# A 16-column projection turned round: its weights stationary, all 256 tokens moving, the result copied out and transposed

## Chip, core and metric

The kernel runs on one core of one Trainium2 chip. The metric is the time of one execution on the device, in microseconds; the median over runs is compared.

## What is computed

Six transformer layers over 256 tokens of width 1024, all in float32. The last two layers (called 0 and 1 below) have a mixer of three branches. One of them is a state-space scan, whose time steps come from sixteen columns of the input projection:

```python
proj = h @ w_in[layer]                      # [256, 1024] @ [1024, IN_DIM]
gm_u, gm_v, ssm_z, ssm_xbc, ssm_dt, ... = split_cols(proj, IN_SIZES)   # ssm_dt: 16 columns
xbc = silu(causal_dwconv(xbc, conv_w, conv_b))
dt = softplus(ssm_dt + dt_bias)             # [256, 16]
y = ssd_scan(xs, dt, a_log, bm, cm, d_skip)
```

Everything in this document happens around `ssm_dt`, the product of 256 tokens x 1024 features with 1024 x 16 weights, once in each of the two layers.

## The kernel before

A float32 product is made of three F32R matmuls. Each operand is split into a high part (ScalarE copies it to F32R) and a low part (VectorE subtracts the high part from the original), and high x high, high x low and low x high are summed in PSUM. The weights stream in as tiles of 128 x 2048: SyncE loads `raw`, ScalarE makes `whi`, VectorE makes `wlo`. Three of each are kept, so the parts of a tile can be made when the tile three before it has been used.

The order of the work is written by a planner, class `Order`. It emits steps, and every engine runs those of its own that have the step's name, in this one order. A projection is a row of steps with a `yield` after each; at each yield `pump` runs, which puts in: a low part if one is due (every second pump), the next piece of the first generator in `pre`, and the next piece of the first generator in `side`. So the side work of the scan (generator `ssm`) is laid between the steps of the big projections, piece by piece. PSUM has eight banks; the side work takes banks 4, 5 and 6 in turn (`aux`), and a semaphore pair per bank (`full`, `empty`) orders writers and readers.

In each of the two layers the order around the change is: the projection of the convolution channels (`col` steps, result `b`), ScalarE's bias step `tap_b`, VectorE's convolution taps `taps_b` and ScalarE's `silu_b` in `pre`; the step `dt`; then the projection `u` (eight `col` steps of twelve matmuls, 256 moving columns each), with the pieces of `ssm` between: `softplus`, four `xs` transposes, `ends`, `cb`, `xde`; then the projection `z` (`tok` steps of six matmuls, 512 moving columns), with `mix`, `state`, `off`, `build`, `decay`, `diag` between.

Step `dt` of TensorE has, for each half of the tokens (t) and each of eight blocks of features (k), the three matmuls with the tokens stationary and the 16 weight columns moving. The result has tokens on the partitions, 16 columns per half, in one bank. VectorE's `softplus` waits for it, adds the bias (L2144), and goes back and forth with ScalarE (Exp, Ln) until `dt` (L2160) and `dA` (L2164) are there. Every line of a helper stands for many uses: L1073 to L1075 are `three`, L1078 is `mm`, L1082 is `tr` (a transpose through TensorE), L1139 to L1141 the matmuls of `col`, L1425 and L1429 are ScalarE's `act` and `copy`, L1768 is the low part of a weight tile, L2063 a convolution tap. In the names of the trace wdh and wdl are the high and low part of the sixteen columns' weights.

Of the kernel before, what the change touches and what calls it, by code (L numbers as in the profile page):

```python
# [164 lines left out]
class Order:  # L165
# [558 lines left out]
    def mixer_2(self, l):  # L724
# [58 lines left out]
        self.step("dt", l, x)  # L783

        def ssm():
            self.counts("stat_v", ("sp0", l))
            self.counts("stat_a", ("sp0", l))
            self.counts("stat_v", ("sp1", l))
            self.counts("stat_a", ("sp1", l))
            self.counts("dtv", l)  # L790
            self.counts("dav", l)
            self.step("softplus", l)
            yield
            for t in range(2):
                for q in range(2):
                    self.aux(("xs", l, t, q))
                    self.counts("xsg", (l, t, q))
                    self.step("xs", l, t, q)
                    yield
            self.aux(("ends", l))  # L800
            self.counts("ea", l)
            self.step("ends", l)
            yield
            self.aux(("cb", l))
            self.step("cb", l)
            yield
            self.counts("xde", l)
            self.step("xde", l)
            for _ in range(3):
                yield  # L810
            for g in range(2):
                self.aux(("state", l, g))
                self.step("state", l, g)
                yield
            for g in range(2):
                self.aux(("off", l, g))
                self.counts("offg", (l, g))
                self.step("off", l, g)
                yield
            seen["xn"] = True  # L820

            def build(n):
                self.counts("built", (l, n))
                self.step("build", l, n)
            build(0)
            yield
            for n in range(8 + 2):
                if n < 7:
                    build(n + 1)
                    yield  # L830
                if n < 8:
                    self.aux(("decay", l, n))
                    self.counts("decays", (l, n))
                    self.step("decay", l, n)
                    yield
                if 1 <= n < 9:
                    self.aux(("diag", l, n - 1))
                    self.step("diag", l, n - 1)
                    yield
# [221 lines left out]
def tensor_program(pe, o, B, sem):  # L1061
# [3 lines left out]
    def activation_ready(x, t, q):  # L1065
        b, n = use["turned", x, t, q]
        p.wait_ge(f"empty{b}", n + 1)
# [237 lines left out]
    def dt(l, x):  # L1305
        b, n = use["dt", l]
        p.wait_ge("wdl", mark["wdl", l])
        p.wait_ge(f"empty{b}", n)
        for t in range(2):
            for k in range(8):  # L1310
                activation_ready(x, t, k // 4)
                lh, ll = B.xh[:, k, 128 * t:128 * t + 128], B.xl[:, k, 128 * t:128 * t + 128]
                last = three(B.bank[b][:, 16 * t:16 * t + 16], lh, ll, B.wdh[:, 16 * k:16 * k + 16],
                             B.wdl[:, 16 * k:16 * k + 16], k == 0 and t == 0, k == 7)
        last.then_inc(sem[f"full{b}"], 1)

    def chan_ready(l, c0, c1):
# [83 lines left out]
    def yparts(l, t, q):  # L1401
# [3 lines left out]
        for k in range(4):  # L1405
# [2 lines left out]
        last.then_inc(sem[f"full{b}"], 1)  # L1408

    does = {"turn_x": turn_x, "tok": tok, "col": col, "row": row, "close": close, "parts": parts, "turn": turn,  # L1410
            "score": score, "probs": probs, "pv": pv, "opart": opart, "turned_up": turned_up, "dt": dt, "xs": xs,
            "ends": ends, "cb": cb, "state": state, "off": off, "decay": decay, "diag": diag, "mix": mix,
            "yparts": yparts}
    for what, *args in o.steps:
# [4 lines left out]
def scalar_program(ac, o, B, sem, ins):  # L1419
# [211 lines left out]
    def silu_b(l, n, j):  # L1631
# [7 lines left out]
            last = act(B.xb[:, c, :], B.xb[:, c, :], ACT.Silu)  # L1639
        last.then_inc(sem["xb"], 1)  # L1640

    def softplus(l):
        a.wait_ge("stat_v", mark["stat_v", ("sp0", l)])
        act(B.ea[:, :, :], B.dA[:, :, :], ACT.Exp).then_inc(sem["stat_a"], 1)
        a.wait_ge("stat_v", mark["stat_v", ("sp1", l)])
        act(B.ea[:, :, :], B.dA[:, :, :], ACT.Ln).then_inc(sem["stat_a"], 1)
# [90 lines left out]
    def mparts(l, j):  # L1737
# [8 lines left out]
            "qk_in": qk_in, "v_in": v_in, "turn": turn, "exp": exp, "probs": probs, "sink": sink, "merge": merge,  # L1746
            "opart": opart, "unturned": unturned, "silu": silu, "hhi": hhi, "tap": tap, "silu2": silu2,
            "gelu_v": gelu_v, "gm_squares": gm_squares, "setup": setup, "tap_b": tap_b, "silu_b": silu_b,
            "softplus": softplus, "xs": xs, "ends": ends, "state": state, "decay": decay, "gelu_u": gelu_u,
            "ya_hi": ya_hi, "z": z, "head_roots": head_roots, "rms_y": rms_y, "sigmoid": sigmoid,  # L1750
            "yparts": yparts, "mparts": mparts}
    for what, *args in o.steps:
# [4 lines left out]
def vector_program(ve, o, B, sem):  # L1757
# [378 lines left out]
                last.then_inc(sem[f"empty{b}"], 1)  # L2136

    def softplus(l):
        b, n = use["dt", l]
        dt, dA, ea, q = B.dt[:, :, :], B.dA[:, :, :], B.ea[:, :, :], B.qst[:, :, :]  # L2140
        v.wait_ge(f"full{b}", n + 1)
        v.wait_ge("small", 16 * (l + 1))
# [422 lines left out]
class Buffers:  # L2565


    def __init__(self, nc, ctx):
        def sb(name, shape, dt=F32, stack=ctx):
            return stack.enter_context(nc.sbuf_tensor(name, shape, dt))  # L2570
# [45 lines left out]
        self.wst = sb("wst", [128, 512])  # L2616
        self.wdh, self.wdl = sb("wdh", [128, 128], F32R), sb("wdl", [128, 128], F32R)
        self.dt, self.dA = sb("dt", [128, 2, 16]), sb("dA", [128, 2, 16])
        self.ea, self.am = sb("ea", [128, 2, 16]), sb("am", [128, 16])
        self.lamt = sb("lamt", [128, 8])  # L2620
        self.qst = sb("qst", [128, 2, 16])
# [184 lines left out]
```

## Time and profile before

| | |
|---|---|
| median of 3 runs | 2547.71 us (2542.21 to 2548.09) |
| profiled execution | 2540.47 us |
| its span, first to last instruction | 2538.6 us |
| TensorE busy (weight loads) | 94% (84%) |
| VectorE, ScalarE, GpSimd busy | 60%, 50%, 19% |
| mean granted TensorE clock | 0.972 of full speed |

The profile is of one execution. An engine's busy share is a mean over stages that have different limits. TensorE matmuls overlap in the pipeline, so what one costs is the distance from start to start and not its duration; the weight loads (PEld) have the clearer starts. A granted clock of 1.00 is 2.4 GHz, 0.50 is 1.2 GHz.

### The profile page before, as it was taken

The page shows a single profiled execution, that of the slowest core. Times are in us where ns is not written, and L with a number is a line of the kernel's source. Part 1 is how long each engine was busy: PE and PEld are TensorE (multiplying, and loading weights), DVE is VectorE, ACT ScalarE, POOL GpSimd, SP SyncE. Part 2 cuts the span into 40 slices and gives each one's busy share as a digit, 9 for nine tenths or more (in the row PEclk, how much of TensorE's full clock was granted, in tenths as well). Part 3 has the DMA queues.
Part 4 walks back from the last instruction along what each step waited for, and adds up shares of the span by engine and source line. Part 5 has one row for each costly group of instructions (what it writes and reads, how often), then busy time and mean ns, then how long its engine had stood idle before and what let it go on. Part 6 is the DMA issues. An engine that isn't in the chain of part 4 may idle for free.

```text
span 2538.6 us, 36912 instructions
## 1 busy us (share of the span) xinstructions
PE 2395.2 (94%) x15388; PEld 2128.6 (84%) x15388; DVE 1513.7 (60%) x2420; ACT 1260.2 (50%) x1806; POOL 481.9 (19%) x368
## 2 busy tenths in 40 slices
PE   7799999999899998999889979999999999989999
PEld 5589978787799777998669969888999898889898
DVE  5465455545654646556465467656677676566766
ACT  4344445455444455444444436555565565454654
POOL 3230042222400333003320001343100013431000
PEclk9799999999999999999889989999999999999999
DMA  6145543333355433555235533434454443344553
GB/s 247 50 171 186 192 166 117 124 142 117 143 189 189 176 133 141 199 183 185 77 117 199 188 140 133 149 121 150 167 186 179 182 163 140 130 150 166 181 185 133
DMA packets 58182, 398.94 MB, mean 157 GB/s; under 512 B 6816, under 2 KB 7072, under 8 KB 11680
## 3 DMA queue, kind: packets, MB, share of 16 engines
q1 hardware_dynamic: 56864, 393.75, 43.0%
q8 instruction: 122, 2.00, 0.3%
q10 hardware_dynamic: 1152, 2.83, 0.3%
q14 instruction: 44, 0.36, 0.0%
HBM read 395.51 MB, written 1.05 MB: 156 GB/s over the span
## 4 chain that ended last, share of the span: by engine, by line
PE 78%; DVE 11%; ACT 7%; issue 2%; POOL 2%; DMA 0%; DVEq 0%; SPq 0%; ACTq 0%; POOLq 0%
PE b L1139 12%; PE b L1141 12%; PE b L1140 12%; PE b L1073 11%; PE b L1074 11%; PE b L1075 11%; PE b L1078 6%; PE b L1082 3%; DVE wlo L1768 3%; ACT whi L1429 2%; ACT S L1426 2%; DVE b L1792 1%; DVE st L1849 1%; DVE b L1847 1%; DVE xl L1799 1%
## 5 line engine op out<-in xcount | busy, mean ns | idle before, releaser
L1768 DVE TENSOR_TENSOR wlo<-raw,whi 128x2048 fp32r<-128x2048 f32 x351 | 831.2, 2373 | 451.4 <-ACT whi L1429 450.6
L1429 ACT ACTIVATE whi<-raw 128x2048 fp32r<-128x2048 f32 x362 | 691.0, 1910 | 355.8 <-PE b L1141 225.9
L1139 PE MATMUL b<-xh,whi 128*128 128x256 f32 x2560 | 727.1, 284 | 3.1 <-DVE wlo L1768 3.1
L1140 PE MATMUL b<-xl,whi 128*128 128x256 f32 x2560 | 722.2, 282 | 0.0
L1141 PE MATMUL b<-xh,wlo 128*128 128x256 f32 x2560 | 722.0, 282 | 0.0
L1139 PEld LDWEIGHTS b<-xh,whi 128*128 128x128 f32 x2560 | 486.1, 190 | 7.9 <-DVE wlo L1768 3.7
L1140 PEld LDWEIGHTS b<-xl,whi 128*128 128x128 f32 x2560 | 486.3, 190 | 2.0
L1141 PEld LDWEIGHTS b<-xh,wlo 128*128 128x128 f32 x2560 | 485.7, 190 | 0.0
L1073 PE MATMUL b<-whi,xh 128*128 128x512 f32 x832 | 345.0, 415 | 32.8 <-DVE xl L1799 16.2
L1074 PE MATMUL b<-wlo,xh 128*128 128x512 f32 x832 | 330.7, 397 | 0.0
L1075 PE MATMUL b<-whi,xl 128*128 128x512 f32 x832 | 329.9, 397 | 0.0
L1073 PE MATMUL b<-whi,oh 128*128 128x512 f32 x656 | 265.4, 405 | 5.6 <-DVE wlo L1768 5.6
L2321 POOL TENSOR_TENSOR wlo<-raw,whi 128x2048 fp32r<-128x2048 f32 x11 | 50.7, 4611 | 1148.1 <-ACT whi L1429 1148.1
L1074 PE MATMUL b<-wlo,oh 128*128 128x512 f32 x656 | 261.5, 399 | 0.0
L1075 PE MATMUL b<-whi,ol 128*128 128x512 f32 x656 | 260.8, 398 | 0.0
L1073 PEld LDWEIGHTS b<-whi,xh 128*128 128x128 f32 x832 | 157.6, 189 | 80.6 <-issue 21.4
L1075 PEld LDWEIGHTS b<-whi,xl 128*128 128x128 f32 x832 | 157.1, 189 | 38.5
L1074 PEld LDWEIGHTS b<-wlo,xh 128*128 128x128 f32 x832 | 157.9, 190 | 33.8 <-issue 1.9
L1073 PEld LDWEIGHTS b<-whi,oh 128*128 128x128 f32 x656 | 127.0, 194 | 32.4 <-DVE wlo L1768 6.9
L1075 PEld LDWEIGHTS b<-whi,ol 128*128 128x128 f32 x656 | 126.3, 192 | 27.7
L1074 PEld LDWEIGHTS b<-wlo,oh 128*128 128x128 f32 x656 | 126.5, 193 | 24.3
L1425 ACT ACTIVATE S<-b 128x256 f32<-128x256 f32 (+1 forms) x104 | 43.4, 418 | 175.8 <-PE b L1141 128.4
(225 smaller groups left out, 2833.6 us busy)
## 6 DMA issues: line engine op xcount, KB each, us to landing
raw<-in_w SPq DMA_DIRECT2D x362, 1024.0 KB, 4.8
gt<-in_rows SPq DMA_DIRECT2D x8, 512.0 KB, 4.0
bt<-in_rows SPq DMA_DIRECT2D x8, 512.0 KB, 5.0
abq<-in_rows ACTq DMA_DIRECT2D x2, 768.0 KB, 5.4
x<-in_x SPq DMA_DIRECT2D x1, 1024.0 KB, 6.7
bc<-in_rows SPq DMA_DIRECT2D x4, 256.0 KB, 5.1
out<-x SPq DMA_DIRECT2D x4, 256.0 KB, 2.0
msk<-in_masks SPq DMA_DIRECT2D x1, 768.0 KB, 7.7
```

The lines of the kernel that those rows point to most:

```text
L1073: pe.matmul(out, lh, rh, start=start, stop=False, skip_group_check=True)
L1074: pe.matmul(out, lh, rl, start=False, stop=False, skip_group_check=True)
L1075: return pe.matmul(out, ll, rh, start=False, stop=stop, skip_group_check=True)
L1078: return pe.matmul(out, l, r, start=start, stop=stop, skip_group_check=True)
L1082: return pe.transpose(out, i, B.ident[0:n, 0:n])
L1139: pe.matmul(out, wh[:, k, cs], ah[:, kk, :], start=kk == 0 and s == 0, stop=False, skip_group_check=True)
L1140: pe.matmul(out, wh[:, k, cs], al[:, kk, :], start=False, stop=False, skip_group_check=True)
L1141: last = pe.matmul(out, wl[:, k, cs], ah[:, kk, :], start=False, stop=final and k == 3, skip_group_check=True)
L1426: return ac.activation(out, i, f, bias=bias, scale=scale, accum_out=acc)
L1429: return ac.activation(out, i, ACT.Copy)
L1768: ve.tensor_tensor(B.wlo[s][:, :], B.raw[r][:, :], B.whi[s][:, :], ALU.subtract).then_inc(sem["loV"], 1)
L2321: ge.tensor_tensor(B.wlo[s][:, :], B.raw[r][:, :], B.whi[s][:, :], ALU.subtract).then_inc(sem["loG"], 1)
```

## The change

The operands of the `dt` matmuls are exchanged. The weights (128 features x 16 columns) are stationary, and all 256 tokens move, so the halves of the tokens fall together: 24 matmuls in place of 48, and the result has the 16 columns on the partitions and the tokens along the row. It must be turned back. ScalarE copies the 16 x 256 values out of PSUM into a new buffer `dtT` (a new step of its own at the place of `dt`), and TensorE transposes the two halves of it into another bank (step `dt_turn`), from which `softplus` now reads. The `ssm` generator begins with a `yield` more, and `dt_turn` and `softplus` stand together after it, so all pieces of `ssm` stand one pump later than before. One use more of `aux` turns the rotation of banks 4, 5, 6 by one from there on.

```diff
--- before.py
+++ after.py
@@ -783,6 +783,9 @@
         self.step("dt", l, x)
 
         def ssm():
+            yield
+            self.aux(("dt_turn", l))
+            self.step("dt_turn", l)
             self.counts("stat_v", ("sp0", l))
             self.counts("stat_a", ("sp0", l))
             self.counts("stat_v", ("sp1", l))
@@ -1307,11 +1310,20 @@
         p.wait_ge("wdl", mark["wdl", l])
         p.wait_ge(f"empty{b}", n)
         for t in range(2):
-            for k in range(8):
-                activation_ready(x, t, k // 4)
-                lh, ll = B.xh[:, k, 128 * t:128 * t + 128], B.xl[:, k, 128 * t:128 * t + 128]
-                last = three(B.bank[b][:, 16 * t:16 * t + 16], lh, ll, B.wdh[:, 16 * k:16 * k + 16],
-                             B.wdl[:, 16 * k:16 * k + 16], k == 0 and t == 0, k == 7)
+            for q in range(2):
+                activation_ready(x, t, q)
+        for k in range(8):
+            ks = slice(16 * k, 16 * k + 16)
+            last = three(B.bank[b][0:16, 0:256], B.wdh[:, ks], B.wdl[:, ks], B.xh[:, k, :], B.xl[:, k, :], k == 0, k == 7)
+        last.then_inc(sem[f"full{b}"], 1)
+
+    def dt_turn(l):
+        b, n = use["dt_turn", l]
+        bd, nd = use["dt", l]
+        p.wait_ge(f"empty{bd}", nd + 1)
+        p.wait_ge(f"empty{b}", n)
+        for t in range(2):
+            last = tr(B.bank[b][:, 16 * t:16 * t + 16], B.dtT[:, 128 * t:128 * t + 128])
         last.then_inc(sem[f"full{b}"], 1)
 
     def chan_ready(l, c0, c1):
@@ -1408,7 +1420,7 @@
         last.then_inc(sem[f"full{b}"], 1)
 
     does = {"turn_x": turn_x, "tok": tok, "col": col, "row": row, "close": close, "parts": parts, "turn": turn,
-            "score": score, "probs": probs, "pv": pv, "opart": opart, "turned_up": turned_up, "dt": dt, "xs": xs,
+            "score": score, "probs": probs, "pv": pv, "opart": opart, "turned_up": turned_up, "dt": dt, "dt_turn": dt_turn, "xs": xs,
             "ends": ends, "cb": cb, "state": state, "off": off, "decay": decay, "diag": diag, "mix": mix,
             "yparts": yparts}
     for what, *args in o.steps:
@@ -1638,6 +1650,11 @@
             c = 4 * n + 2 * j + s
             last = act(B.xb[:, c, :], B.xb[:, c, :], ACT.Silu)
         last.then_inc(sem["xb"], 1)
+
+    def dt(l, x):
+        b, n = use["dt", l]
+        a.wait_ge(f"full{b}", n + 1)
+        copy(B.dtT[:, :], B.bank[b][0:16, 0:256]).then_inc(sem[f"empty{b}"], 1)
 
     def softplus(l):
         a.wait_ge("stat_v", mark["stat_v", ("sp0", l)])
@@ -1746,7 +1763,7 @@
             "qk_in": qk_in, "v_in": v_in, "turn": turn, "exp": exp, "probs": probs, "sink": sink, "merge": merge,
             "opart": opart, "unturned": unturned, "silu": silu, "hhi": hhi, "tap": tap, "silu2": silu2,
             "gelu_v": gelu_v, "gm_squares": gm_squares, "setup": setup, "tap_b": tap_b, "silu_b": silu_b,
-            "softplus": softplus, "xs": xs, "ends": ends, "state": state, "decay": decay, "gelu_u": gelu_u,
+            "dt": dt, "softplus": softplus, "xs": xs, "ends": ends, "state": state, "decay": decay, "gelu_u": gelu_u,
             "ya_hi": ya_hi, "z": z, "head_roots": head_roots, "rms_y": rms_y, "sigmoid": sigmoid,
             "yparts": yparts, "mparts": mparts}
     for what, *args in o.steps:
@@ -2136,7 +2153,7 @@
                 last.then_inc(sem[f"empty{b}"], 1)
 
     def softplus(l):
-        b, n = use["dt", l]
+        b, n = use["dt_turn", l]
         dt, dA, ea, q = B.dt[:, :, :], B.dA[:, :, :], B.ea[:, :, :], B.qst[:, :, :]
         v.wait_ge(f"full{b}", n + 1)
         v.wait_ge("small", 16 * (l + 1))
@@ -2616,6 +2633,7 @@
         self.wst = sb("wst", [128, 512])
         self.wdh, self.wdl = sb("wdh", [128, 128], F32R), sb("wdl", [128, 128], F32R)
         self.dt, self.dA = sb("dt", [128, 2, 16]), sb("dA", [128, 2, 16])
+        self.dtT = sb("dtT", [16, 256])
         self.ea, self.am = sb("ea", [128, 2, 16]), sb("am", [128, 16])
         self.lamt = sb("lamt", [128, 8])
         self.qst = sb("qst", [128, 2, 16])
```

## Rows read from the trace of the kernel before

**Rows 1.** The page: busy time, the chain that ended last by engine.
```profile
PE 2395.2 (94%) x15388; PEld 2128.6 (84%) x15388; DVE 1513.7 (60%) x2420; ACT 1260.2 (50%) x1806; POOL 481.9 (19%) x368
...
PE 78%; DVE 11%; ACT 7%; issue 2%; POOL 2%; DMA 0%; DVEq 0%; SPq 0%; ACTq 0%; POOLq 0%
```

**Rows 2.** Groups by line and shape, whole span: count, busy us, mean ns, idle before.
```profile
L1074 PE MATMUL b<-wdl,xh 128*128 128x16 f32 x32 | 8.8, 276 | 0.0
```

**Rows 3.** Timeline of weight loads, layer 0: start us, us, what; releaser in brackets.
```profile
1564.24 0.19 PEld L1140 LDWEIGHTS b<-xl,whi 128*128 128x128 f32 x1
...
1564.48 0.19 PEld L1073 LDWEIGHTS b<-wdh,xh 128*128 128x128 f32 x1
...
1568.17 0.29 PEld L1073 LDWEIGHTS b<-wdh,xh 128*128 128x128 f32 x1
...
1571.33 0.33 PEld L1139 LDWEIGHTS b<-xh,whi 128*128 128x128 f32 x1
...
1575.12 0.19 PEld L1139 LDWEIGHTS b<-xh,whi 128*128 128x128 f32 x1
```

**Rows 4.** The same, layer 1: start and end of the block and of its tail.
```profile
2075.09 0.19 PEld L1073 LDWEIGHTS b<-wdh,xh 128*128 128x128 f32 x1
...
2080.68 0.33 PEld L1139 LDWEIGHTS b<-xh,whi 128*128 128x128 f32 x1
...
2083.66 0.19 PEld L1141 LDWEIGHTS b<-xh,wlo 128*128 128x128 f32 x1
```

**Rows 5.** Busy time and granted clock (third from the end) in stretches of both layers.
```profile
1564.48:1567.90 3.42, 3.42 (x34) 3.42 (x32) 0.00 (x0) 0.00 (x0) 0.00 (x0) 1.00 0.19 81
1568.20:1571.33 3.13, 3.13 (x17) 3.13 (x16) 0.00 (x0) 0.00 (x0) 0.00 (x0) 0.50 0.00 0
...
1575.12:1587.62 12.50, 12.50 (x111) 12.50 (x109) 10.58 (x15) 10.63 (x16) 9.19 (x8) 1.00 0.28 93
```

**Rows 6.** Timeline of VectorE, layer 0.
```profile
1571.58 0.26 DVE L2144 TENSOR_TENSOR dt<-b,small 128x16 f32<-128x16 f32 x2 [10.65 <-PE b L1075]
...
1574.75 2.29 DVE L1768 TENSOR_TENSOR wlo<-raw,whi 128x2048 fp32r<-128x2048 f32 x1
1576.95 5.79 DVE L2063 SCALAR_TENSOR_TENSOR xb<-b,col,xb 128x255 f32<-128x255 f32 x12
1583.40 2.56 DVE L1768 TENSOR_TENSOR wlo<-raw,whi 128x2048 fp32r<-128x2048 f32 x1 [0.66 <-ACT whi L1429]
```

**Rows 7.** Timeline of ScalarE, layer 0.
```profile
1561.96 1.02 ACT L1425 ACTIVATE xb<-b,col 128x256 f32<-128x256 f32 x2 [0.86 <-PE b L1141]
...
1573.86 0.23 ACT L1425 ACTIVATE ea<-dA 128x32 f32<-128x32 f32 x1
...
1579.06 1.28 ACT L1425 ACT_TABLE_LOAD   x1
1580.35 0.72 ACT L1425 ACTIVATE xb<-xb 128x256 f32<-128x256 f32 x2
...
1581.46 1.91 ACT L1429 ACTIVATE whi<-raw 128x2048 fp32r<-128x2048 f32 x1
```

**Rows 8.** Timeline of weight loads, layer 0: around `xs`, and where z begins.
```profile
1575.85 0.46 PEld L1082 LDWEIGHTS b<-cst,xb 128*128 128x128 f32 x4
1576.27 0.19 PEld L1139 LDWEIGHTS b<-xh,whi 128*128 128x128 f32 x1
...
1587.62 0.19 PEld L1073 LDWEIGHTS b<-whi,xh 128*128 128x128 f32 x1
```

**Rows 9.** The same, at the first decay matmul.
```profile
1606.35 0.97 PEld L1078 LDWEIGHTS b<-cst,PT 128*128 128x128 f32 x8 [1.13 <-DVE PT L2189]
```

**Rows 10.** The same, around a plain F32 matmul of 512 columns.
```profile
1592.59 0.42 PEld L1078 LDWEIGHTS b<-xn,btok 128*128 128x128 f32 x2
...
1593.68 0.19 PEld L1074 LDWEIGHTS b<-wlo,xh 128*128 128x128 f32 x1 [0.24 <-issue]
```

**Rows 11.** The same, after the score matmuls of the attention.
```profile
1694.58 0.19 PEld L1139 LDWEIGHTS b<-xh,whi 128*128 128x128 f32 x1 [0.33 <-issue]
```

## Prediction, made before the changed kernel was timed

> **What bounds the kernel now.** I read the page first. TensorE is busy 94% of the span, and the chain that ended last is 78% TensorE, 11% VectorE, 7% ScalarE [rows 1]. So TensorE time taken away comes off the end, unless another engine becomes late. The groups by shape then show the work that the change replaces: three groups of 32 matmuls (one stands for them), each 16 columns wide, under 128-column weight loads [rows 2]. Their mean of 276 ns is a latency. The price is the distance from one start to the next, so I went to the timeline of the weight loads in both layers.
>
> In layer 0 the block begins at 1564.48 and the next projection at 1571.33 [rows 3]: 6.85 us for 48 matmuls. The first 33 loads take 3.69 us (1564.48 to 1568.17), 0.112 us each; the last 15 take 3.16 us, 0.21 us each. The stretches say why: the granted clock is 1.00 (2.4 GHz) until 1567.90 and 0.50 (1.2 GHz) from 1568.20 [rows 5]. It stays low past the block, until about 1575, over the next projection's matmuls, which are 256 columns wide. In layer 1 the block runs from 2075.09 to 2080.68, 5.59 us, and only its last loads and the tail up to 2083.66 are slow [rows 4]. Before the fall the engine had issued nothing but 16-column matmuls since 1564.48; in 12.50 us of 256-column matmuls with transposes between them the clock stayed at 1.00 [rows 5].
>
> Who waits for the block? VectorE sat idle 10.65 us until it ended, and had the low part of a weight tile (wlo, 1574.75) and twelve convolution taps (1576.95) queued behind [rows 6]. TensorE did not wait for VectorE: the weight low part for the z projection was ready at 1585.96, and z began at 1587.62 [rows 6, 8]. There is one TensorE wait later in the same side chain: 1.13 us before the first decay matmul, for VectorE's `PT` [rows 9].
>
> **The change part by part.**
>
> *Matmuls.* 48 become 24 with 256 moving columns. The nearest row is the projection beside it, same types and moving width: 0.118 us apart (from 1564.24 to 1564.48 two) [rows 3]. 24 x 0.118 = 2.83 us. No row has only 16 stationary columns. Below: with a shorter load the spacing might be 0.107 us (256 columns at 2.4 GHz), 0.26 us less per layer. Above: the plain F32 matmul; one with 512 columns took the two loads from 1592.59 to 1593.68 less 0.23 us (two times 0.118) for the 512-column L1073 matmul between, 0.86 us, so 0.43 us for 256 [rows 10]. The types stay F32R, so I take 0.118. Block: layer 0 6.85 - 2.83 = 4.02 us, layer 1 5.59 - 2.83 = 2.76 us.
>
> *The slow tail.* Layer 0: from 1571.33 to 1575.12 stand 18 loads, 3.79 us, at full clock 18 x 0.118 = 2.12: 1.67 us. Layer 1: 2080.68 to 2083.66, 14 loads, 2.98 against 1.65: 1.33 us. I count both as gained, 3.00 us, since beside 256-column matmuls no row of this stretch has a fall.
> The rows show the clock falling with TensorE busy 3.42 of 3.42 us [rows 5]. The Trainium skill, "TensorE: Matmul & The Clock Gate", section "Part 1: The HAM clock gate", says that the gate follows how busy the PE has been. By that alone the falls are not the 16-column matmuls' doing and the tails would stay: the sum would be 3.0 us smaller. The trace agrees only as far as the clock has two levels.
>
> *Transposes.* Two per layer, 16 partitions in. Four 128x128 ones take from 1575.85 to 1576.27, 0.42 us [rows 8], so two cost 0.21 us, with a hand-over 0.22; total 0.44. Above, the nearest row with fewer than 128 rows in use is the score block, where 0.33 us of issue idle follows it [rows 11]; twice that, 0.66 us per layer, is the upper bound.
> The Trainium skill, "TensorEngine Tiling (Array Packing)", section "Tiling Modes", says that a change of tiling mode drains the engine. The 0.33 us agrees in kind. Were it paid into and out of both new parts, the sum would be 4 x 0.33 x 2 = 2.6 us smaller.
>
> *The ScalarE copy.* 16x256 from PSUM; the nearest row is the bias step, two operations of 128x256 from PSUM in 1.02 us, so at most 0.5 us [rows 7]. It is queued ahead of the bias step of the last convolution channels, which ran at 1561.96 while the block was still to come [rows 7]. Now that step waits. TensorE itself does not wait for the copy: the transposes come two projection steps (24 matmuls, 2.83 us) later.
>
> *The chain behind the copy.* This is the new queue, and I follow it for layer 0. Block ends 1564.48 + 2.83 = 1567.31, copy 1567.6 to 1568.0 or 1568.1. Bias step 1.02 us: 1569.0. Half of the twelve taps, now ahead of the softplus, 5.79 / 2 = 2.9: 1571.9. Softplus as before, 1571.58 to 1574.75 = 3.2 us: 1575.1; ScalarE has its last part 2.5 us into it (1573.86 + 0.23), so is free at 1574.45. Then on ScalarE: bias 1.02, `xs` copy 0.5, table load 1.28, silu 0.72, `xs` copy 0.5, high part of the next weights 1.9: 1580.4. VectorE's low part 2.3: 1582.65 [rows 6, 7]. The low part before it is no longer stuck behind the softplus; it can run at 1561.1 (1561.96 - 0.86, where ScalarE's high part ends) instead of 1574.75. TensorE comes to z at 1587.62 - (4.02 + 1.67 - 0.22) = 1582.15. So it waits 0.5 us, and in layer 1, whose new code is the same, 0.5 us again. This takes back 1.0 us.
>
> *One side step later.* The added yield puts every later side step one projection step further back. The TensorE wait for `PT` was for VectorE, which still had other results and a wlo to work off [rows 9]; with one more step of six 512-column matmuls between, 1.4 us if each takes two of the 0.118 us, it should go: 1.13 us per layer, bounds 0 and 1.13. I take 1.0, 2.0 in all. The extra bank use turns the rotation of banks 4, 5, 6; it meets each bank after the same number of uses, and I cost it at nothing. If one such bank is late, it costs about 0.5 us.
>
> *Sum.* 4.02 + 2.76 + 3.00 - 0.44 - 1.0 + 2.0 = 10.3 us. The profiled execution took 2540.47 us (span 2538.6 plus 1.9 around it), so 2530.2 against it. The median of the runs is 2547.71, 7.2 us above the profiled one, which the profile cannot explain, and I take the 10.3 off the median: 2537.4 us. A measurement of this kernel tells 0.3%, 7.6 us, from no change, so the border is 2540.1.
>
> **The rivals.**
>
> A, the forecast: 2537.4, own range 2534 to 2541. Chance 0.60.
>
> B, the chain holds TensorE. The chain computed above ends within 0.5 us of TensorE's arrival, so every microsecond by which it is longer costs one per layer. Two more engine hand-overs and an unsplit pair of taps make 1.5 us, and then the decay wait stays as well: 10.3 - 2 x 1.4 - 2.0 = 5.5, 2542.2. For it: twelve small operations on two engines one behind the other. Against: VectorE has 10.65 us idle to give. Chance 0.20.
>
> C, the clock falls all the same, since the new matmuls too are unlike the projection's: 16 stationary columns in place of 128. The tails stay, 3.0 us, and half of each new block runs at 0.21 us, 12 x 0.095 x 2 = 2.3 us: 10.3 - 5.3 = 5.0, 2542.7. For it: no row has a thin stationary side. Against: the block is only 2.83 us among full ones. Chance 0.10.
>
> D, the other side: the matmuls with 16 stationary columns do not run at the 0.118 us pace but at the plain F32 one, 0.43 us. Each block is 24 x 0.31 = 7.5 us longer, 15.0 in all, while the 1.0 us wait for the chain goes: 10.3 + 1.0 - 15.0 = -3.7, 2551.4; with the drains (2.6) and the decay waits (2.0) on top 2556, which is slower. From 0.118 + 10.3 / 48 = 0.33 us per matmul the gain is gone, from 0.49 us it is measurably slower without more. Chance 0.04.
>
> E, it changes too little to see: the blocks shorten, but waits later in the layers, those at the attention's bank hand-overs above all, take it back, and 2 to 3 us are left, 2545. Against: these chains start from TensorE's own results. Chance 0.06.
>
> **How the numbers follow.** The range 2532 to 2545 takes in A, B, C and E, 3 us below the forecast's lower side for the shorter load (0.5), the later low-clock stretches and the spread of the median, and leaves D out. Faster than 2540.1: A but for its upper edge, 0.53, and a little of B and C, 0.04: 0.57. Slower: D with its extras, 0.03, and 0.01 for an unseen wait: 0.04. The rest, 0.39, is within 0.3%.
>
> **What the changed profile would show.** Right: 24 matmuls of 256 columns per layer 0.118 us apart, granted clock 1.00 from the block to z, VectorE's wlo before the softplus, ScalarE's bias step right behind the copy, z beginning about 18.2 us after the block's first load (23.14 before in layer 0), no `PT` wait. Wrong: a spacing over 0.13 us (D), a clock of 0.50 (C), a wait for wlo of over 1 us before z or one at `cb` (B), longer waits past the mixer (E).

## The result, and the profile after

| | before | changed |
|---|---|---|
| median | 2543.04 us (6 runs, 2539.98 to 2548.09) | 2531.35 us (6 runs, 2526.93 to 2534.05) |
| profiled execution | 2540.47 us | 2531.4 us |
| its span | 2538.6 us | 2529.6 us |
| mean granted clock | 0.972 | 0.976 |

The ratio of changed to before is 0.9947, interval 0.9935 to 0.9959: 0.53% faster. The forecast was 2537.4 us, range 2532 to 2545. The direction was right; the time lies just below the range. Of all executions counted in this document one was slow: the third of early_turned took 3876.15 us at a mean granted clock of 0.556; it stays out of that kernel's ratio and moves its median by 0.04 us.

The profile's page of the changed kernel, busy time and the chain that ended last [rows 1]:

```profile
PE 2384.8 (94%) x15344; PEld 2116.6 (84%) x15344; DVE 1509.2 (60%) x2420; ACT 1259.6 (50%) x1808; POOL 478.2 (19%) x368
...
PE 74%; DVE 11%; ACT 7%; issue 5%; POOL 2%; DMA 0%; POOLq 0%; SPq 0%; DVEq 0%; ACTq 0%
```

The shares hardly move; a change of this size is not seen there. TensorE's busy time fell by 10.4 us, the span by 9.0. The timeline of the weight loads shows the place. Layer 0, then layer 1 [rows 3, 4, 8, 9]:

```profile
1563.87 0.10 PEld L1076 LDWEIGHTS b<-xh,wdh 128*16 128x16 f32 x1
1563.99 0.09 PEld L1077 LDWEIGHTS b<-xl,wdh 128*16 128x16 f32 x1
...
1566.68 0.19 PEld L1142 LDWEIGHTS b<-xh,whi 128*128 128x128 f32 x1
...
1569.40 0.19 PEld L1144 LDWEIGHTS b<-xh,wlo 128*128 128x128 f32 x1
1569.72 0.20 PEld L1085 LDWEIGHTS b<-cst,dtT 16*128 16x128 f32 x2
1569.95 0.19 PEld L1142 LDWEIGHTS b<-xh,whi 128*128 128x128 f32 x1
...
1582.01 0.19 PEld L1076 LDWEIGHTS b<-whi,xh 128*128 128x128 f32 x1 [0.20 <-DVE wlo L1785]
...
1588.39 1.09 PEld L1081 LDWEIGHTS b<-wst,og 128*128 128x128 f32 x8
1589.95 0.30 PEld L1081 LDWEIGHTS b<-xn,btok 128*128 128x128 f32 x2 [0.47 <-POOL xn L2433]
...
1601.63 0.97 PEld L1081 LDWEIGHTS b<-cst,PT 128*128 128x128 f32 x7
...
2088.03 0.19 PEld L1076 LDWEIGHTS b<-whi,xh 128*128 128x128 f32 x1 [0.21 <-DVE wlo L1785]
```

Its windows, the block and from the block to z, layer 0 and layer 1 [rows 5]:

```profile
1563.87:1566.68 2.81, 2.81 (x26) 2.26 (x25) 0.00 (x0) 0.00 (x0) 0.00 (x0) 1.00 0.99 397
1566.68:1582.01 15.33, 15.32 (x131) 14.97 (x128) 9.81 (x23) 12.61 (x20) 5.64 (x5) 1.00 0.03 11
2069.88:2072.70 2.82, 2.82 (x27) 2.26 (x26) 0.00 (x0) 0.00 (x0) 0.00 (x0) 1.00 1.00 398
2072.70:2088.03 15.33, 15.32 (x131) 14.97 (x128) 9.82 (x23) 12.62 (x20) 5.64 (x5) 1.00 0.03 13
```

The block takes 2.81 us in both layers (6.85 and 5.59 before), and the clock is 1.00 from it to z: no slow tail. From the block's first load to z are 18.14 and 18.15 us (23.14 and 21.55 before). The wait for `PT` at the first decay matmul, 1.13 us in [rows 9], is gone. New is one of 0.47 us for GpSimd's `xn`, before the first state matmul; the distance to the load before it is longer by 0.57 than without a wait. The two engines of the side chain, VectorE and then ScalarE [rows 6, 7]:

```profile
1560.52 2.29 DVE L1785 TENSOR_TENSOR wlo<-raw,whi 128x2048 fp32r<-128x2048 f32 x1 [0.20 <-ACT whi L1441]
1568.30 2.94 DVE L2080 SCALAR_TENSOR_TENSOR xb<-b,col,xb 128x255 f32<-128x255 f32 x6 [5.49 <-ACT xb L1437]
1571.16 0.24 DVE L2161 TENSOR_TENSOR dt<-b,small 128x16 f32<-128x16 f32 x2
...
1574.20 0.19 DVE L2181 TENSOR_TENSOR dA<-dt,am 128x32 f32<-128x32 f32 x1
1574.59 2.94 DVE L2080 SCALAR_TENSOR_TENSOR xb<-b,col,xb 128x255 f32<-128x255 f32 x6 [0.20 <-ACT xb L1437]
1579.40 2.55 DVE L1785 TENSOR_TENSOR wlo<-raw,whi 128x2048 fp32r<-128x2048 f32 x1 [1.87 <-ACT whi L1441]
```

```profile
1567.00 0.37 ACT L1441 ACTIVATE dtT<-b 16x256 f32<-16x256 f32 x1 [6.51 <-PE b L1078]
1567.28 0.99 ACT L1437 ACTIVATE xb<-b,col 128x256 f32<-128x256 f32 x2
...
1577.47 1.91 ACT L1441 ACTIVATE whi<-raw 128x2048 fp32r<-128x2048 f32 x1
```

This is the order that the prediction laid out: copy, bias step, half of the taps, softplus, the other half, and at the end the weight parts that z waits for. The low part that used to stand behind the softplus now runs at 1560.52.

### The profile page after: what moved, and what is told of

Its sections match the earlier page's. It is cut to its first block, busy times and chain, and to the rows that moved or that the text cites. A ratio compares the mean times of both kernels' runs of the same rounds, so it can differ in the third digit from the quotient of the medians.

```text
span 2529.6 us, 36826 instructions
## 1 busy us (share of the span) xinstructions
PE 2384.8 (94%) x15344; PEld 2116.6 (84%) x15344; DVE 1509.2 (60%) x2420; ACT 1259.6 (50%) x1808; POOL 478.2 (19%) x368
## 4 chain that ended last, share of the span: by engine, by line
PE 74%; DVE 11%; ACT 7%; issue 5%; POOL 2%; DMA 0%; POOLq 0%; SPq 0%; DVEq 0%; ACTq 0%
PE b L1142 11%; PE b L1144 11%; PE b L1143 11%; PE b L1076 11%; PE b L1077 10%; PE b L1078 10%; PE b L1081 6%; PE b L1085 3%; ACT whi L1441 2%; DVE wlo L1785 2%; ACT S L1438 2%; DVE b L1809 1%; DVE st L1866 1%; DVE b L1864 1%; DVE xl L1816 1%
```

## Experiments

Each ran with the kernel before on the same chip; the kernels of one batch share those runs. "To z" is from the block's first load to the first load of z, layer 0 and layer 1, in the one profiled execution; "low" is the time at granted clock 0.50 in it.

| kernel | median us (runs) | before us (runs) | ratio, interval | to z | low |
|---|---|---|---|---|---|
| changed_again | 2531.95 (5) | 2545.77 (20) | 0.9947, 0.9935 to 0.9959 | 18.14, 18.14 | 0, 0 |
| shift_only | 2542.75 (11) | 2545.77 | 0.9990, 0.9980 to 0.9999 | 24.71, 24.69 | 10.2, 10.2 |
| split_narrow | 2538.72 (9) | 2545.77 | 0.9977, 0.9966 to 0.9987 | (split) | 3.4, 3.4 |
| no_yield | 2533.89 (5) | 2545.77 | 0.9960, 0.9947 to 0.9972 | 19.87, 19.85 | 0, 0 |
| before_2 | 2546.15 (1) | 2546.07 (9) | | 23.17, 23.09 | 6.8, 6.8 |
| before_3 | 2540.13 (1) | 2546.07 | | 21.53, 23.09 | 3.4, 6.8 |
| early_turned | 2536.61 (5) | 2546.07 | 0.9965, 0.9952 to 0.9979 | (earlier block) | 0, 0 |
| early_yield | 2531.08 (5) | 2546.07 | 0.9943, 0.9930 to 0.9957 | (earlier block) | 0, 0 |
| eight_copies | 2539.66 (10) | 2543.45 (13) | 0.9984, 0.9974 to 0.9993 | 19.98, 19.98 | 0, 0 |
| half_width | 2532.53 (4) | 2543.45 | 0.9957, 0.9942 to 0.9972 | 18.23, 18.23 | 0, 0 |
| state_later | 2534.22 (4) | 2543.45 | 0.9962, 0.9947 to 0.9977 | 18.15, 18.14 | 0, 0 |
| before_4 | 2540.19 (1) | 2543.45 | | 21.51, 23.09 | 3.4, 6.8 |

### changed_again: the changed kernel once more

> The changed kernel once more, for the size of the gain and a second trace. Theory (the sum of the prediction as the first trace corrects it: blocks 6.8 us, slow tails 3.0, less 0.64 for transposes, 1.0 for the wait before z, 0.3 to 0.6 gained by the step shift): 9 us, so a ratio of 0.9965, and layer gains at z of 5.0 and 3.4 us against the first trace of before, 23.14 and 21.55 us from block to z becoming 18.1 both times. Rival: the gain really is what the medians say, 11.7 us or more (ratio 0.9954 or less); then a second trace has to show several microseconds more outside the two mixers or in the clock.

The ratio is the same to the fourth place, and so are the distances to z. The distances are those of the theory (18.1), the ratio is on the rival's side of 0.9954. But this second profiled execution took 2533.01 us, 1.6 more than the first, and does not show the several microseconds more that the rival asked for. The kernel before stands at 2545.77 us over 20 runs, so the gain by these medians is 13.8 us; by the six runs of the result it is 11.7 us.

### before_2, before_3, before_4: the kernel before, profiled again

> The kernel before once more, for a second trace of the two blocks. Theory (the first trace of before was a mild case; where the low clock begins in the block and how long it lasts varies from execution to execution, as the 10.2 us of low clock in each layer of the shift-only kernel show): more low clock around the two blocks than the 10.2 us (6.8 + 3.4) of the first trace, blocks plus tails longer than its 8.5 + 6.9 us excess-included 10.64 us (layer 0, block start to 18 wide matmuls on) and 8.57 us (layer 1, 14 on). Rival (the first trace is typical and the 13 us of gain come from elsewhere): 10.2 us again, and the difference to the changed kernel then lies outside the mixers.

> The same, third trace. Theory and rival as for the second; over the three traces the mean time from the block's first load to z's is above 22.4 us, the mean of the first trace's 23.14 and 21.55, and where it is longer the low clock around the block is longer by as much time as 0.45 of it.

> The kernel before, one more look. Theory (the low clock round the narrow blocks is there in every execution and only its length changes, 3.4 to 10.2 us per layer): a stretch of 3.4, 6.8 or 10.2 us begins 2.5 to 6 us after each block's first load, and block to z is 21.5, 23.1 or 24.7 us. Rival (the profiled executions that had it were unlucky): no low clock there, 20 us to z.

Windows of before_2 and then of before_3, layer 0, at full and at low clock:

```profile
1567.08:1570.60 3.52, 3.52 (x35) 3.52 (x33) 0.00 (x0) 0.00 (x0) 0.00 (x0) 1.00 0.16 68
1570.60:1577.40 6.80, 6.80 (x34) 6.80 (x34) 1.57 (x9) 1.74 (x3) 0.00 (x0) 0.50 0.00 0
```

```profile
1563.01:1568.40 5.39, 5.39 (x51) 5.39 (x50) 0.00 (x0) 0.00 (x0) 0.00 (x0) 1.00 0.12 47
1568.40:1571.80 3.40, 3.40 (x18) 3.40 (x18) 1.72 (x11) 1.74 (x3) 0.00 (x0) 0.51 0.00 0
```

The low clock is there every time, for 3.4 or 6.8 us, as the theories had it. Of the eight distances to z in four profiled executions of the kernel before, five are 23.1 and three 21.5 us, mean 22.5. The kernel's total times spread from 2536.9 to 2548.5 us. Of the 6.0 us between before_2 and before_3, 4.07 arise ahead of the block, which begins at 1567.08 and 1563.01: ahead of everything that the change touches. Starts from 1562.6 to 1567.6 occur with changed kernels too. The profiled execution of [rows 1], 2540.47 us, was on the low side of the spread.

### shift_only: the old matmuls, the side work one step later

```diff
         def ssm():
+            yield
+            self.ring += 1
             self.counts("stat_v", ("sp0", l))
```

> The kernel before with the added yield and the turned bank rotation alone; the 48 narrow matmuls, no copy, no transposes. Theory (the parts add up): the block stays 5.6 to 6.9 us and the clock falls in it; the wait for the decay matmul (1.13 us) goes but a wait of GpSimd's xn before the first state matmul may come, so a gain of 0 to 2 us in all, ratio 0.9992 to 1.0000. Rival (the scheduling is the gain and the matmuls are cover): 5 us or more, ratio 0.998 or less.

Alone, the shift takes the `PT` wait away: the second half of z takes 15.78 us in place of 16.62, 0.84 us per layer, with the same matmuls in it. The low clock stays, and in this execution it was longer. Windows in layer 0 and layer 1:

```profile
1569.20:1579.40 10.20, 10.20 (x49) 10.20 (x49) 3.81 (x15) 2.65 (x5) 0.00 (x0) 0.50 0.02 6
...
2081.20:2091.40 10.20, 10.20 (x49) 10.20 (x49) 4.09 (x16) 2.65 (x5) 0.00 (x0) 0.50 0.01 6
```

The gain by the medians, 3.0 us (interval 0.3 to 5), holds the 1.7 us of the two waits; the rival's 5 us stand at the end of the interval. The wait for `xn` that the theory thought possible did not come: the first half of z takes 16.25 us, as before.

### eight_copies: 128 moving columns under the same loads

```diff
-                last = three(B.bank[b][:, 16 * t:16 * t + 16], lh, ll, B.wdh[:, 16 * k:16 * k + 16],
-                             B.wdl[:, 16 * k:16 * k + 16], k == 0 and t == 0, k == 7)
+                rh = B.wdh[:, 16 * k:16 * k + 16].unsqueeze(1).broadcast_to([128, 8, 16])
+                rl = B.wdl[:, 16 * k:16 * k + 16].unsqueeze(1).broadcast_to([128, 8, 16])
+                out = B.bank[b][:, 128 * t:128 * t + 128].rearrange("p (r c) -> p r c", r=8)
+                last = three(out, lh, ll, rh, rl, k == 0 and t == 0, k == 7)
...
-            last = ve.tensor_tensor(B.dt[:, t, :], B.bank[b][:, 16 * t:16 * t + 16], B.sm("dtb"), ALU.add)
+            last = ve.tensor_tensor(B.dt[:, t, :], B.bank[b][:, 128 * t:128 * t + 16], B.sm("dtb"), ALU.add)
```

> The kernel before, but each of its 48 matmuls moves its sixteen weight columns eight times over (128 moving columns, the result stands eight times in the bank); the tokens stay stationary and the order of the work is that of before. Theory (it is the 16 moving columns under full-size loads after which the clock falls): the pace stays 0.112 us, so each block takes 5.4 us, with a granted clock of 1.00 in it and up to z; from the block's first load to z 5.4 + 14.7 = 20.1 us in both layers, where three profiles of the kernel before have 21.5 to 23.2 (mean 22.6). That is 2.5 us per layer less, 5.0 in all, about 2541 against 2546, ratio 0.998. Rival (the clock's fall is due to something else in that place, such as what goes before the block): low clock again, 3.4 to 10.2 us per layer, 21.5 to 24.7 us to z, ratio 1.000.

The theory holds almost to the tenth: 19.98 us to z in both layers (20.1 expected), ratio 0.9984 (0.998 expected). Its windows, block and block to z in layer 0, then the same in layer 1:

```profile
1567.40:1572.77 5.37, 5.37 (x51) 5.37 (x50) 0.00 (x0) 0.00 (x0) 0.00 (x0) 1.00 0.13 56
1572.77:1587.39 14.62, 14.62 (x128) 14.62 (x128) 12.59 (x25) 11.55 (x19) 9.56 (x7) 1.00 0.23 73
2075.35:2080.71 5.36, 5.36 (x51) 5.36 (x49) 0.00 (x0) 0.00 (x0) 0.00 (x0) 1.00 0.13 55
2080.71:2095.33 14.62, 14.62 (x128) 14.62 (x127) 12.58 (x25) 11.54 (x19) 9.57 (x7) 1.00 0.20 73
```

Same loads, same count, same pace (0.112 us), eight times the columns, and the clock does not fall. So the fall belongs to the 16-column matmuls, and costs 22.5 - 20.0 = 2.5 us per layer on average, more than half of what the change gains up to z (22.5 - 18.1 = 4.4). The median gains 3.8 us and not the 5.0 expected: behind z's first load this kernel newly waits for GpSimd's `xn`, 0.57 us per layer (see below). In both kernels the profile counts TensorE busy for the whole block (3.42 of 3.42 us in [rows 5], 5.37 of 5.37 here). The Trainium skill, "TensorE: Matmul & The Clock Gate", section "Part 1: The HAM clock gate", says that the gate follows how busy the PE has been; as far as the profile's busy time goes, the two kernels do not differ in that, and the trace does not bear out that reading of the rule.

### split_narrow: the old block in two halves

```diff
         for n in range(3):
+            if n == 2:
+                self.aux(("dt", l))
+                self.step("dt", l, x, 0)
...
-        self.aux(("dt", l))
-        self.step("dt", l, x)
+        self.step("dt", l, x, 1)
...
-        for t in range(2):
+        for t in (half,):
...
```

> The kernel before with its 48 narrow matmuls in two halves: tokens 0 to 127 before the last convolution projection, tokens 128 to 255 at the old place. Same matmuls, same total. Theory (the clock falls because of 5.4 us of narrow matmuls in a row): each half takes 24 x 0.112 = 2.7 us at granted clock 1.00 and no tail follows; time from the start of the second half to z is 17.8 us plus waits; gain 3.1 us in layer 0 and 1.5 in layer 1 against the first trace of before, ratio about 0.998. Rival (the clock fell at those places for another reason, or it falls with half the narrow matmuls too): low clock in or just behind the halves, and a gain below 1 us.

The first half (24 matmuls, 2.68 us) stands ahead of the last convolution projection. Windows of it, of what follows, and of the low stretch, layer 0:

```profile
1554.17:1556.85 2.68, 2.68 (x27) 2.68 (x25) 2.54 (x7) 1.44 (x3) 0.00 (x0) 1.00 1.00 404
1556.85:1558.30 1.45, 1.45 (x14) 1.45 (x14) 1.38 (x5) 1.34 (x2) 0.00 (x0) 1.00 0.95 384
1558.30:1561.70 3.40, 3.40 (x19) 3.40 (x18) 3.33 (x5) 1.60 (x3) 0.00 (x0) 0.50 0.05 22
```

The first half is still followed by 3.4 us of low clock, which begins 1.45 us after it, on 256-column matmuls; the second half is followed by none. In layer 1 it is the same. A shorter narrow block brings at most a shorter low clock (3.4 us per layer where before has 3.4 or 6.8), but does not end it. So the theory's ratio came out (0.9977 against 0.998) and its mechanism did not: 24 narrow matmuls are enough for a fall. The profiled stretch does not account for the ratio either: from the last convolution projection to v, both halves counted, it takes 66.2 us per layer, and 66.8 on average in the four executions of the kernel before, 1.1 us in both layers, where the medians differ by 7.1.

### no_yield: the changed kernel without the step later

```diff
         def ssm():
-            yield
             self.aux(("dt_turn", l))
```

> The changed kernel without the added yield: transposes and softplus one projection step (12 matmuls, 1.4 us) after the block, and the softplus ahead of the convolution taps on VectorE again. Theory (the yield keeps TensorE off VectorE's and GpSimd's side chain but is worth little): no TensorE wait for the ScalarE copy (copy ends 0.7 us after the block's end, transposes come 1.4 us after), the 1.13 us wait for PT is back, the 0.68 us wait for GpSimd's xn is gone, so within 1 us per layer of the changed kernel, 0.2 to 0.8 slower. Rival (without the yield the transposes wait for the copy and the side chain reaches z later): 1.5 us or more per layer slower.

Three waits appear in the timeline of the weight loads, layer 0, and the same in layer 1:

```profile
1574.00 0.19 PEld L1141 LDWEIGHTS b<-xh,whi 128*128 128x128 f32 x1 [1.09 <-DVE wlo L1784]
...
1580.20 0.41 PEld L1080 LDWEIGHTS b<-xb 128*128 128x128 f32 x3 [0.80 <-ACT xb L1436]
...
1601.25 0.41 PEld L1080 LDWEIGHTS b<-cst,PT 128*128 128x128 f32 x3 [1.13 <-DVE PT L2205]
```

To z it takes 19.87 us, 1.73 more than the changed kernel. With the softplus in front, VectorE comes late to the low part that TensorE wants in u, and ScalarE late to `xb`, which `cb` reads. The transposes do not wait for the copy: the distance from load to load round them is the same 0.55 us. So the recorded rival had the size right, and the wait in the wrong place. It is the prediction's rival B, the chain that holds TensorE, with its waits at u and `cb` and not before z; the added yield is what keeps it away. By the traces the yield is worth 1.73 + 0.84 - 0.57 = 2.0 us per layer here, 4.0 in all; the medians differ by 1.9, with intervals that overlap.

### early_turned and early_yield: the new block one projection earlier

Both put the step `dt` ahead of the last convolution projection, as in split_narrow but whole; early_turned is no_yield with this edit, early_yield the changed kernel with it.

```diff
         for n in range(3):
+            if n == 2:
+                self.aux(("dt", l))
+                self.step("dt", l, x)
...
-        self.aux(("dt", l))
-        self.step("dt", l, x)
```

> The changed kernel with the block of 24 matmuls and the ScalarE copy moved ahead of the last convolution projection, and without the added yield: transposes and softplus stand one projection step after that projection. Theory (what is left in the changed kernel is the side chain behind the block: 0.5 us before z and 0.68 us before state): the copy no longer holds the bias step, but the softplus is again ahead of wlo and the taps; the first wait is gone, PT's 1.13 us is back: within 1 us per layer of the changed kernel. Rival (the softplus ahead of wlo costs what it cost without the yield, 1.7 us per layer at z, wherever the block stands): 3 us slower than the changed kernel, ratio near 0.996.

> The same early block, with the added yield kept. Theory: VectorE's taps need not wait for a bias step behind the copy, so the whole chain before z is 2.8 us or more earlier, no wait before z, state or PT: 1 us per layer faster than the changed kernel, 2 us in all, ratio 0.9939. Rival (the chain was not what TensorE waited for): the same waits and the same ratio of 0.9947 as the changed kernel.

The order of the softplus matters more than the place of the block: early_turned has waits like those of no_yield (1.02 us at the low part, 1.01 at `cb`, 1.32 at `PT`, as distances between loads), early_yield none of over 0.45 us between block and v. Its windows of the two halves of z:

```profile
1584.47:1600.72 16.25, 16.25 (x75) 12.24 (x74) 12.75 (x15) 11.84 (x12) 8.42 (x7) 1.00 0.52 178
1600.72:1616.50 15.78, 15.78 (x90) 13.54 (x88) 9.81 (x18) 6.86 (x7) 5.00 (x4) 1.00 0.37 137
```

It has lost the `xn` wait too (16.25 us in place of 16.82), and the wait before z. From the last convolution projection to z, the block counted in both, it takes 29.22 us where the changed kernel takes 29.50, so up to v it is 0.85 us per layer faster, 1.7 in all: near the 2 us of its theory. The medians are too coarse to show it (2531.08 against 2531.95). For early_turned the rival was right: 31.01 us over the same stretch, 1.5 more per layer than the changed kernel, and a ratio of 0.9965.

### half_width: thin stationary side, 128 moving columns

```diff
-            last = three(B.bank[b][0:16, 0:256], B.wdh[:, ks], B.wdl[:, ks], B.xh[:, k, :], B.xl[:, k, :], k == 0, k == 7)
+            for t in range(2):
+                ts = slice(128 * t, 128 * t + 128)
+                last = three(B.bank[b][0:16, ts], B.wdh[:, ks], B.wdl[:, ks], B.xh[:, k, ts], B.xl[:, k, ts],
+                             k == 0 and t == 0, k == 7)
```

> The changed kernel, but with 48 matmuls of 128 moving columns (half of the tokens each) under the sixteen stationary columns in place of 24 of 256. Theory (the pace of a matmul with a thin stationary side is set by its moving columns, since the block of 24 went at 0.118 us with loads of 0.09 us): 0.059 us each, a block of 2.9 us, the time of the changed kernel, 2532. Rival (each pair of load and matmul has a floor of about 0.11 us, as the 16-column matmuls of before have): 5.4 us per block, 5.2 us more in all, 2537. The clock: 1.00 throughout by both; if small matmuls as such bring it down, 0.50 within the block and a tail behind it, 3 to 7 us more still.

Windows of the block and up to z, layer 0:

```profile
1567.58:1570.52 2.94, 2.94 (x51) 2.92 (x50) 0.00 (x0) 0.00 (x0) 0.00 (x0) 1.00 1.01 418
1570.52:1585.80 15.28, 15.28 (x132) 14.96 (x129) 9.82 (x23) 12.62 (x20) 5.64 (x5) 1.00 0.02 8
```

48 matmuls in 2.94 us, 0.061 us each: the pace goes by the moving columns, and there is no floor of 0.11 us under a thin load. The floor that the old block had came with its 128-column loads. A load of 16 columns is shown with 0.09 us, one of 128 with 0.19. The Trainium skill, "TensorE: Matmul & The Clock Gate", section "LDWEIGHTS (loading the stationary operand)", says that a load's time goes by its columns alone; the direction agrees, the size does not (half, not an eighth).

### state_later: the state matmuls one pump later

```diff
             self.step("xde", l)
-            for _ in range(3):
+            for _ in range(4):
                 yield
```

> The changed kernel with one pump more between xde and the first state matmul, so that the state matmul and all that follows it in the side work stand one z step later. Theory (the 0.67 us wait of TensorE for GpSimd's xn product is what the moved side work newly costs): that wait is gone in both layers, the first z half takes 16.25 us in place of 16.82, 1.1 to 1.3 us less in all, 2530.7 against 2531.9. Rival (it is only moved): a wait of 0.5 us or more turns up at a later side step before v, and the time stays at 2531.9.

The rival was right that the wait is only moved, though it comes behind z, in v, and not before v. The `xn` wait is gone (16.06 us for the first half of z), and z ends 1.5 us sooner, but 0.9 of it are side matmuls that moved back, 0.7 of these the eight for `S` that now stand behind z, and there a new wait stands, in the timeline of the weight loads:

```profile
1632.90 0.41 PEld L1081 LDWEIGHTS b<-xs,S 128*128 128x128 f32 x3
1634.04 0.74 PEld L1081 LDWEIGHTS b<-cst,PT 128*128 128x128 f32 x6 [0.72 <-DVE PT L2206]
```

At the last weight load of v it is 0.2 us behind the changed kernel, in both layers (75.9 against 75.7 us from z's first load). A wait removed by one more step can come back a projection later.

## Why the prediction came out as it did

*The base failed.* The step of the prediction was: "The median of the runs is 2547.71, 7.2 us above the profiled one, which the profile cannot explain, and I take the 10.3 off the median". That median was of three runs, and two of them lay at the top of the kernel's spread. Over six runs it is 2543.04. The forecast lies 6.05 us too high: 4.67 are this base, and 1.4 are the gain (10.3 forecast, 11.7 by these medians). With 2543.04 as the base it would have been 2532.7, inside the range. From profile to profile the forecast was 2530.2 against 2531.4 measured. The working says that the range begins 3 us below the forecast's lower side, 2534; that is 2531, the range as given begins at 2532, and 2531.35 lies between them.

*The gain, term by term*, from the two profiled executions (layer 0 + layer 1, us):

| term | forecast | measured |
|---|---|---|
| block | 4.02 + 2.76 | 4.04 + 2.77 |
| slow tail | 1.67 + 1.33 | 1.67 + 1.33 (none left) |
| two transposes | -0.22 - 0.22 | -0.43 - 0.43 |
| wait before z | -0.5 - 0.5 | -0.28 - 0.28 |
| `PT` wait gone | +1.0 + 1.0 | +0.85 + 0.85 |
| `xn` wait new | 0 | -0.57 - 0.57 |
| sum up to v | 10.3 | 8.95 |

The transposes: from the load before them (1569.40) to the one after (1569.95) are 0.55 us, of which 0.118 is the usual distance. That is twice the forecast and inside its bound of 0.66. The wait before z: 0.39 us between loads, less 0.118. The rest of the span, outside block to v, gives 0.1 us in sum, and there stretches of low clock elsewhere came and went (in layer 0 -0.67 us behind v, in layer 1 +0.15, ahead of the block +0.61).

*The chain* behaved as laid out. The block began 0.61 us earlier than in the kernel before (1563.87 against 1564.48), so the times are compared from the block's first load: the softplus ran from 7.3 to 10.5 us (forecast 7.4 to 10.6), the high part ended at 15.5 (15.9), and z began at 18.14 (18.17). This hit is not two errors that happened to cancel: z waits for the low part, which ended at 18.1, so the 0.21 us that the transposes took beyond the forecast came off the wait before z.

*The step that failed beside the base* is "The added yield puts every later side step one projection step further back", with "it should go": the shift was booked as pure gain, 2.0 us, and 0.56 came. The `PT` wait did go, 1.7 us, and shift_only shows that the shift alone does it. But a wait for `xn`, one step earlier in that chain, was put at nothing without a word, and took 1.14 us. The working did not ask whether GpSimd would be done when TensorE came 3 to 5 us sooner. The shift alone does not bring this wait: shift_only takes 16.25 us for the first half of z. Nor does it need the shift: eight_copies, which has none, takes 16.81 and 16.82 us, and split_narrow 16.72 and 16.74, while no_yield, which has none either, takes 16.25. Part of the cause is in the timeline of GpSimd, and of VectorE beside it, in the changed kernel:

```profile
1582.94 1.04 POOL L2426 TENSOR_TENSOR xs<-xs,dt 128x512 f32<-128x512 f32 x1
...
1585.06 2.97 POOL L2426 TENSOR_TENSOR xs<-xs,dt 128x512 f32<-128x512 f32 x1
1588.00 1.90 POOL L2433 TENSOR_TENSOR xn<-xs,ea 128x1024 f32<-128x1024 f32 x1
...
1584.57 2.56 DVE L1785 TENSOR_TENSOR wlo<-raw,whi 128x2048 fp32r<-128x2048 f32 x1 [1.84 <-ACT whi L1441]
```

The same operation takes 1.04 and 2.97 us. Over the second VectorE runs a low part, and about 0.9 us after that has ended the product ends too. eight_copies shows the same with `xn`, 3.96 us beside a low part at 1588.81. Where `xn` starts first it keeps its time, and the low part takes 3.92 us in place of 2.29, as in no_yield:

```profile
1584.12 1.91 POOL L2432 TENSOR_TENSOR xn<-xs,ea 128x1024 f32<-128x1024 f32 x1
...
1584.26 3.92 DVE L1784 TENSOR_TENSOR wlo<-raw,whi 128x2048 fp32r<-128x2048 f32 x1 [1.52 <-ACT whi L1440]
```

The Trainium skill, "Trainium Architecture — The Big Picture", section "What this means for kernel authors", says that VectorE and GpSimd contend for one shared port pair, which one of them holds alone; the trace agrees, with these numbers.

The slow product alone does not make TensorE wait. early_yield has it too:

```profile
1586.74 2.97 POOL L2427 TENSOR_TENSOR xs<-xs,dt 128x512 f32<-128x512 f32 x1
```

What decides is when `xn` has ended against when TensorE comes, both counted from z's first load:

| kernel | `xn` ends | first load that reads it | wait per layer |
|---|---|---|---|
| before | 2.2 | 4.97 | none |
| no_yield | 3.5 | 4.97 | none |
| eight_copies | 5.5 | 5.65 | 0.57 |
| shift_only | 6.0 | 7.38 | none |
| early_yield | 7.1 | 7.38 | none |
| changed | 7.9 | 7.94 | 0.57 |

The wait is the excess of the first half of z over 16.25 us. For eight_copies the profile names no releaser; there the wait is put down to `xn` because the load follows `xn`'s end by 0.1 us.

In the changed kernel the chain ran 0.8 us later against z than in early_yield, and the slow product adds 1.9 us. Without these 1.9 us `xn` would have ended at about 6.0, ahead of TensorE; this is an estimate, for no run here set the meeting of the two engines by itself.

*The rivals.* C is out: the clock is 1.00 from the block to z in every kernel with the new operands. D is out: 0.118 us, and 0.061 with half the columns. B did not come, and no_yield shows that it was near (1.7 us per layer). Of E there is only the 1.1 us for `xn`, inside the mixer and not at the attention's hand-overs that E named. Of the prediction's reading "beside 256-column matmuls no row of this stretch has a fall", split_narrow shows the limit: a fall can begin 1.45 us into them, behind narrow ones.

*Left open.* By profiled executions the gain is 9.1 us (13.1 if before_2 is set against changed_again, both with a late start), by medians 11.7 to 13.8, and 10 to 17 by the interval of the ratio. Three of the four profiled executions of the kernel before took about 2540 us, while its medians lie between 2543 and 2546. The mean granted clocks agree: 0.972 over its four profiled executions, 0.970 over the 42 of the experiments, and 0.974 over the eleven of the changed kernel, profiled or not. So the kernel before had more low clock in the executions that were not profiled. Whether it lay round the blocks, as shift_only's 10.2 us suggests, or elsewhere, can't be said from these runs, and the 7.1 us of split_narrow are as open.

## What to carry to other kernels

Where a product has few columns, let these be the stationary side and the long side move: the count halves here, the pace follows the moving columns, and the matmuls no longer bring the clock down for the work that comes after them. Take a forecast's difference from the profile, but not its base from three runs whose spread (5.9 us) is over half of the gain. When a step is moved, or an engine comes sooner, follow every engine of the chain to the next meeting point, and look at what else it meets there; compare times from the same event, here z's first load, and not from the start of the span.

## What was not expected of the hardware

- A low clock of 3.4 us began 1.45 us after a block of 24 matmuls of 16 columns, on wide matmuls (split_narrow), and 3.4, 6.8 or 10.2 us of it began in or right behind each of the ten blocks of 48 that were profiled; with eight times the columns and all else alike there was none.
- Two transposes with 16 rows in use cost 0.43 us of TensorE's time, 0.2 of it ahead of the first.
- A GpSimd product of 128x512 took 1.04 us alone and 2.97 us beside a VectorE subtraction of 2.56 us; where GpSimd started first, it kept its time and the subtraction took 3.92 us.
- A load of 16 columns took 0.09 us where one of 128 took 0.19, and still 48 of them went by in 2.94 us.
